# Attention over the prompt moved into the projection stage of a fused two-layer kernel, and the samples' recurrence into the prompt's recurrence stage

## The reference, cut to what matters

```python
def even_mixer(x, prev_row, S0, k_buf, v_buf, start_pos, prm, i):
    proj = x @ w_in
    pr = proj[..., :RWKV_COLS]
    ...
    mixed = pr + prm['tshift_mu'][i] * (shifted - pr)
    y_a, S = rwkv7_mixer(mixed, S0, ...)
    q, ks, vs = jnp.split(proj[..., RWKV_COLS:], ...)
    y_b, k_new, v_new = swa_mixer(q, ks, vs, k_buf, v_buf, start_pos, prm['attn_sinks'][i], prm['rel_bias'])
    out = jnp.concatenate([y_a, y_b], axis=-1) @ prm['w_out'][i]
```

## Time and profile before

| what | value |
|---|---|
| median of 3 runs | 1638.11 us (1632.55 to 1643.83) |
| the profiled execution: span of its instructions | 1637.2 us (its own time from outside is not recorded apart) |
| PE busy, mean granted clock | 1449.6 us (89%), 0.927 |
| DVE, ACT, POOL busy | 642.2, 366.8, 207.0 us |
| input transposed, from 0 to | 26.8 us |
| `project`, products, to | 331.2 us |
| `attend`, to | 448.3 us |
| `rwkv_chunks`, to | 641.4 us |
| `mix_out`, experts, pooling, experts, to | 1637.2 us |

### The profile page before, as it was taken

One profiled execution on the slowest core, in us unless ns is written; L12 is line 12 of the kernel. 1 busy time (PEld: TensorE's weight loads), 2 busy tenths in 40 slices (PEclk: granted clock), 3 DMA queues, 4 the chain that ended last, 5 costly groups with the idle time before them and its releaser, 6 DMA issues. The chain is left out here.

```text
span 1637.2 us, 26246 instructions
## 1 busy us (share of the span) xinstructions
PE 1449.6 (89%) x10111; PEld 889.8 (54%) x10112; DVE 642.2 (39%) x1022; ACT 366.8 (22%) x789; POOL 207.0 (13%) x266
## 2 busy tenths in 40 slices
PE   6999999966779998999749999994994699999968
PEld 4566666645668895445424444443794344444423
DVE  1122553069245562867551111115795211111117
ACT  1333110066523332111201111111231111111111
POOL 4000000000054332110001101005000101010040
PEclk9999999988689999999959999996797799999989
DMA  6673110041020003000378796776005688786353
GB/s 194 133 284 132 29 26 26 0 115 22 9 51 4 4 4 114 28 26 27 114 261 298 261 332 235 271 240 245 1 28 202 235 270 303 277 281 223 146 217 120
DMA packets 137055, 236.96 MB, mean 145 GB/s; under 512 B 20178, under 2 KB 100035, under 8 KB 136682
## 3 DMA queue, kind: packets, MB, share of 16 engines
q1 hardware_dynamic: 113458, 151.01, 29.0%
q0 software_dynamic: 16880, 60.49, 10.0%
q10 hardware_dynamic: 6624, 24.12, 3.7%
HBM read 178.92 MB, written 58.21 MB: 145 GB/s over the span
## 5 line engine op out<-in xcount | busy, mean ns | idle before, releaser
L2299 PE MATMUL ex_pb<-ew_w_gate_up,ex_xT 128*128 x736 | 330.0, 602 | 6.0 <-issue 3.7
L298 PE MATMUL pj_pb<-pj_xT,pj_w 128*128 128x348 f32 (+3 forms) x960 | 282.1, 455 | 0.8 <-ACT pj_xT L322 0.8
L298 PEld LDWEIGHTS pj_pb<-pj_xT,pj_w 128*128 128x128 f32 (+1 forms) x960 | 178.8, 186 | 101.9 <-ACT pj_xT L322 0.8
L2299 PEld LDWEIGHTS ex_pb<-ew_w_gate_up,ex_xT 128*128 128x128 f32 x736 | 138.0, 192 | 165.2 <-issue 164.1
L2282 PE MATMUL ex_pb<-ew_w_down,ex_hiddenT 128*128 x368 | 165.7, 593 | 3.4 <-ACT ex_hiddenT L2369 3.4
L2492 DVE TENSOR_TENSOR ex_hidden<-ex_hidden,ex_pb 128x256 f32<-128x256 f32 x46 | 19.4, 421 | 324.6 <-ACT ex_hidden L2364 324.6
L2282 PEld LDWEIGHTS ex_pb<-ew_w_down,ex_hiddenT 128*128 128x128 f32 x368 | 66.3, 190 | 69.9 <-issue 69.9
L2487 DVE COPY ex_y_rows<-ex_pb 128x512 f32<-128x512 f32 x46 | 31.8, 692 | 134.5 <-PE ex_pb L2282 134.5
L430 DVE SCALAR_TENSOR_TENSOR mixed<-pj_pb,v_mu,mixed 128x347 f32<-128x347 f32 (+3 forms) x42 | 24.0, 572 | 145.7 <-ACT mixed L372 145.6
L2364 ACT ACTIVATE ex_hidden<-ex_pb 128x256 f32<-128x256 f32 x46 | 17.7, 386 | 261.4 <-PE ex_pb L2299 261.4
L2242 POOL COPY ex_tokens_now<-ex_token_of_slot 128x1 uint32 (+1 forms) x48 | 9.6, 200 | 451.3 <-PE ex_pb L2271 399.3
(11 more groups left out here) (423 smaller groups left out, 2061.2 us busy)
## 6 DMA issues: line engine op xcount, KB each, us to landing
ew_w_gate_up<-in_w_ex_gate SPq DMA_DIRECT2D x32, 1024.0 KB, 8.4
ew_w_gate_up<-in_w_ex_up SPq DMA_DIRECT2D x32, 1024.0 KB, 11.0
ew_w_down<-in_w_ex_down SPq DMA_DIRECT2D x32, 1024.0 KB, 13.1
scratch_slots_out<-ex_y_rows ACTq DMA_DIRECT2D x46, 512.0 KB
scratch_slots_out<-pj_tmp POOLq DMA_DIRECT2D x4, 4096.0 KB, 16.0
scratch_x_stored<-x_rows SPq DMA_DIRECT2D x16, 512.0 KB
pj_w<-in_w_in SPq DMA_DIRECT2D x7, 1024.0 KB, 10.5
minus_kk_then_y<-in_x_prompt SPq DMA_DIRECT2D x8, 512.0 KB
```

The costliest lines, as they stand in the source:

```text
L298: last = nc.tensor.matmul(product(at)[:, 0:tn], w[:, s % NW, k, c0:c0 + mrows], xT[:, k, x0:x0 + tn], start=(k == 0), stop=(k == KD - 1))
L2299: last = mm(pb[:, 2 + u, :], xT[:, u, k, :], w[:, k, :], start=(k == 0), stop=(k == KD - 1))
```

## The change

`project` and `attend` become one stage, `project_attend`. The tiles are computed in another order: keys and values first (thirds 0 to 5), then queries (6 to 17), then keys of the recurrence (18 to 29), and so on; so the first 6 tiles are plain and 14 mixed ones follow. Slab 0 now holds 256 columns where it held 192, and the gathered slabs are 1 and 2. The products have two banks (4 and 5) up to third 47 and four after it. The steps of the attention are tied to the third `at` after whose products they are issued: PE's scores of block n in thirds 16 + 3n and 17 + 3n (a half of the heads each, two banks for both), the exponentials in 18 + 3n and 19 + 3n, DVE's half of the normalising in 19 + 3n and ACT's in 20 + 3n, transposes in 21 + 3n and 22 + 3n, outputs in 22 + 3n and 23 + 3n. The scores have two buffers, laid over the array of the decay sums; bias and transposed probabilities lie over the array of the rates. The samples' attention stands at single thirds from 18 to 38; the norms of the keys follow in thirds 41 to 46, decay and rate from 47. The reciprocal (L411 of before) is cut into three parts for each tile. The samples' recurrence goes into `rwkv_chunks`: its transposes and copies into step 0, its 18 DVE operations three to a step into steps 1 to 6, its loads behind the loads of `w_out` on SP. The diff, cut to its core:

```diff
-def project(nc, io, pr, A, B, U, pq, vec, keep, const):
+def project_attend(nc, io, pr, A, B, U, pq, vec, keep, const):
-    slabs = [(NR, WL + AL + GL, ((0, WL + AL, 12), (WL + AL, GL, 13)))]
-    slabs += [(HW * j, HW, ((0, P, 2 * j), (P, P, 2 * j + 1))) for j in (2, 3, 0, 1, 4, 5)]
-    slabs += [(QC + HW * j, HW, ((0, P, 14 + 2 * j), (P, P, 15 + 2 * j))) for j in range(3)]
+    slabs = [(QC + HW * j, HW, ((0, P, 14 + 2 * j), (P, P, 15 + 2 * j))) for j in (2, 0, 1)]
+    slabs += [(HW * j, HW, ((0, P, 2 * j), (P, P, 2 * j + 1))) for j in (2, 3, 0)]
+    slabs += [(NR, WL + AL + GL, ((0, WL + AL, 12), (WL + AL, GL, 13)))]
+    slabs += [(HW * j, HW, ((0, P, 2 * j), (P, P, 2 * j + 1))) for j in (1, 4, 5)]
-    Q_SLABS = (7, 8)
+    Q_SLABS = (1, 2)
+    V_ROWS = 7
+    SCORES, EXPS, TURNED = 16, 18, 21
+    S_KEYS, S_SCORES, S_ROWS, S_MAX, S_EXP, S_NORM, S_PROBS, S_OUT, S_TAKEN = (18, 21), 24, 27, 27, 29, 30, 33, 36, 38
+    SQUARES, NORMS, LORA, SMALL = 37, 41, 46, 47
+    INVERSES = tuple(42 + c if c < 9 else 43 + c for c in range(12))
+    SUMS, KEYS = (48, 50, 52, 54), (51, 55, 56, 57)
+    WIDE = 48
+        def bank_of(at):
+            return 4 + (at % 4 if at >= WIDE else at % 2)
...
@@ SP @@
+            load_slab(1)
             for v in range(KVH):
...
-            load_slab(1)
+            load_slab(2)
...
+            sp.wait_ge(s_tr, TILES)
+            sp.dma_start(kc, io["cache_swa_k"][0].rearrange("b t h d -> t b (h d)")).then_inc(q["k_in"], 16)
             sp.wait_ge(s_bw, 16)
...
+            load_slab(3)
             sp.wait_ge(q["v_tr"], 1)
...
+            load_slab(4)
...
+            for k in range(5, len(slabs)):
+                load_slab(k)
@@ PE @@
+            def prompt_attention(at):
+                n, step = of_block(at, TURNED)
+                if step == 0:
+                    transposes(n, 0)
+                    transposes(n, 1)
+                elif step == 1:
+                    transposes(n, 2)
+                    transposes(n, 3)
+                    output(n, 0)
+                    output(n, 1)
+                elif step == 2:
+                    output(n, 2)
+                    output(n, 3)
+                n, step = of_block(at, SCORES)
+                if step in (0, 1):
+                    scores(n, step)
...
+                    if at in (WIDE + 2, WIDE + 3):
+                        pe.wait_ge(q["y"], NT)
+                        pe.wait_ge(q["sy"], 1)
+                    else:
+                        before = at - 4 if at >= WIDE + 4 else at - 2
...
+                    prompt_attention(at)
+                    sample_attention(at)
...
@@ ACT, after its part of the product @@
+                    n_, step = of_block(at, TURNED)
+                    if step in (0, 1):
+                        probs(n_, 2 * step)
+                        probs(n_, 2 * step + 1)
+                    elif step == 2:
+                        take_y(n_)
+                    n_, step = of_block(at, EXPS)
+                    if step in (0, 1):
+                        exps(n_, step)
+                    elif step == 2:
+                        normalise(n_)
@@ DVE, after its part of the product @@
+                    n_, step = of_block(at, SCORES)
+                    if step in (0, 1):
+                        masked_scores(n_, step)
+                    n_, step = of_block(at, EXPS + 1)
+                    if step == 0:
+                        normalise(n_)
@@ rwkv_chunks, PE (called at six places of step 0) @@
+            def sample_rows(j):
+                if j == 0:
+                    pe.wait_ge(q["pre"], 1)
+                else:
+                    pe.wait_ge(q["rows_cp"], j)
+                for t in range(4):
+                    last = nc.tensor.transpose(pb[0:NS, 2, P * t:P * t + P], sample_cols(j, t), ident[:, :])
@@ rwkv_chunks, DVE @@
+            def samples(n, place):
+                k = 3 * (n - 1) + place
+                if 0 <= k < 18:
+                    sample_step(k // 9, k % 9)
                 if n:
                     take_a_by_state(n - 1, 1)
+                    samples(n, 0)
                 take_z(n, 2)
                 take_by_r(n, 1)
                 take_x(n, 2)
                 if n + 1 < NT:
                     take_a_by_b(n + 1)
+                if n:
+                    samples(n, 1)
                 take_z(n, 3)
                 take_x(n, 3)
                 if n + 1 < NT:
                     take_b_k_by_a(n + 1)
+                if n:
+                    samples(n, 2)
                 take_z(n, 4)
@@ rwkv_chunks, SP, behind the two loads of w_out @@
+            for j in range(6):
+                sp.wait_ge(q["rows_cp"], j + 1)
+                sp.dma_start(scr[j], vrow[j]).then_inc(q["rows_wr"], 16)
+            sp.wait_ge(q["rows_wr"], 96)
+            for half in range(2):
...
```

More of the change, by code:

```diff
@@ L204, in project @@
         s_slots = m.sem("slots_zeroed")
+        names = ("sink v_tr v_cp bias_rd sc masked neg ex inv prob_v prob_a ptr pcp o y out k0"
+                 " k_in v_in s_in kt ktc qc ssc sscc tr mx sex spr tr2 tr2c so sy").split()
+        q = {k: m.sem(f"at_{k}") for k in names}
+        n_small = 16 * (3 + 2 * NS)
         block = m.block()
@@ new lines, in take_xT, with copy_qkv @@
+        def take_xT(eng, copy, par):
+            for i in range(par, TILES, 2):
+                n = P if i < NT else 2 * NS
+                eng.wait_ge(s_tr, i + 1)
+                src = pb[:, 2 * par:2 * par + 2, :].rearrange("p b (k t) -> p (b k) t", k=4)[:, :, 0:n]
+                copy(xT[:, :, 1 + P * i:1 + P * i + n], src).then_inc(s_xT[par], 1)
+        def copy_qkv(eng, copy, at):
+            t0, _, n, _ = thirds[at % 3]
+            eng.wait_ge(s_mm, at + 1)
+            copy(pq[:, tiles[at // 3][3] - 14, 1 + t0:1 + t0 + n], product(at)[:, 1:1 + n]).then_inc(s_cp[at % 2], 1)
@@ new lines, in rate, with norm @@
+            def rate(t, cut):
+                t0, tn = cuts[cut]
+                act.wait_ge(s_small, small + 1)
+                small_taken(nc.scalar.activation(B[:, t, t0:t0 + tn], pb[:, small_bank(small), 0:tn], ACT.Sigmoid,
+                                                 bias=vec["iclr_a0"][:, t:t + 1]))
+            def norm(t, cut):
+                t0, tn = cuts[cut]
+                act.wait_ge(s_small, small + 1)
+                small_taken(nc.scalar.activation(A[:, t, t0:t0 + tn], pb[:, small_bank(small), 0:tn], ACT.Sqrt))
@@ new lines, in _ @@
+            for i, (_, _, mrows, tile) in enumerate(tiles):
+                for third, (t0, n_prompt, n, _) in enumerate(thirds):
+                    at = 3 * i + third
+                    if i < PLAIN:
+                        if at % 2:
+                            copy_qkv(dve, nc.vector.tensor_copy, at)
+                    else:
+                        dve.wait_ge(s_now, at - 3 * PLAIN + 1)
+                        mu = vec["mu"][0:mrows, tile:tile + 1]
+                        out = pr[0:mrows, tile, t0:t0 + n]
+                        last = stt(out=out[:, 0:n_prompt], in0=product(at)[:, 0:n_prompt], scalar=mu, in1=out[:, 0:n_prompt],
+                                   op0=ALU.mult, op1=ALU.add)
+                        if n > n_prompt:
+                            last = stt(out=out[:, n_prompt:], in0=product(at)[:, 1 + n:1 + n + NS], scalar=mu, in1=out[:, n_prompt:],
+                                       op0=ALU.mult, op1=ALU.add)
+                        last.then_inc(s_mix, 1)
+                    if at == V_ROWS:
+                        value_rows()
+                    n_, step = of_block(at, SCORES)
[4 more added lines that the diff above has]
+                        normalise(n_)
+                    if at == 3 * PLAIN:
+                        sample_queries()
+                    if at == S_SCORES:
+                        sample_scores()
+                    if at == S_MAX:
+                        sample_max()
+                    if at == S_NORM:
+                        sample_normalise()
+                    if at == S_PROBS:
+                        sample_probs()
+                    if at in INVERSES:
+                        inverse_norm(*divmod(INVERSES.index(at), 3))
+                    if at in SUMS:
+                        sums(SUMS.index(at))
+                    if at in KEYS:
+                        keys(KEYS.index(at))
@@ L1331, in _ @@
             last.then_inc(q["so"], 1)
+            pe.wait_ge(q["ydr"], 16)
+            pe.wait_ge(q["asc"], 2 * NT)
+            for t in range(4):
+                last = nc.tensor.transpose(pb[:, 1, NS * t:NS * t + NS], yr[:, P * t:P * t + P], ident[0:NS, 0:NS])
+            last.then_inc(q["ytr"], 1)
         @block.vector
```

869 lines of the change are left out of this document (407 added, 462 removed).

## The result

The changed kernel takes 1601.5 us (median of four, 1593.6 to 1602.9) against 1637.7 us (1632.6 to 1643.8): ratio 0.977, 95% interval 0.973 to 0.980. The forecast was 1596 us in a range of 1584 to 1614. The profiled execution has a span of 1601.1 us, 36.1 less than before and 5.6 more than the 1595.5 forecast for it.

The account below looks back on a forecast made before the run. The prediction took PE to bound the projection and the latency of a chain over three engines the attention. From 1637.2 us, -50.7 for the merging and +9.0 for the recurrence gave 1595.5, forecast as 1596, range 1584 to 1614.

Parts of the forecast that it names:

- part 3: Recurrence stage: grows by 9.0 us from taking in the samples' recurrence.
- Part 1: Attention stage: disappears from the path with one barrier, 117.1 us.
- Part 2: Merged stage: PE's attention work at full clock, switches, slab 0 and the end cost 66.4 us; net gain 50.7.
- (a): Start of the recurrence: a load of ACT's exponential table stands on the path, +1.3 us.
- (b): Recurrence step 0: six added groups of four transposes and ACT copies, +2.0 us (0 to 6).
- (d): Recurrence steps 1 to 6: 18 samples' DVE operations cost 0.7 us a step at place 0, +4.2 (0 to 22).
- (c): Recurrence step 1: DVE's operation at place 0 waits for loads through memory, +1.5 us (0 to 8).
- (e): Recurrence start: PE enters at half clock as before, 0 us (to -3.5).
- Rival 1: Recurrence stage becomes bound by DVE: 1620 us at worst, chance 0.09.
- Rival 2: Merged stage: PE waits about 3 us in thirds B and C of each block; middle 1622 us, chance 0.05.
- Rival 3: Merged stage: PE waits out each block's chain, 35 us a block instead of 20.2; 1714 us, chance 0.03.
- Rival 4: Merged stage: a semaphore puts the attention's tail behind the products; gain only 20 us, 1617 us, chance 0.03.

Follow-up runs that it names:

- run 8: Changed kernel with each block's transposes two thirds earlier, PE's scores before transposes, ACT's exponentials before copies: 1672.7 us against 1644.8 for the kernel before, single execution.
- run 1: Changed kernel with the samples' output of seven of eight samples left out: the recurrence begins at 394.57, 8.0 us earlier.
- run 2: Changed kernel with the samples' scores issued in two thirds and their output in four, nothing left out: 1596.6 us, ratio 0.974.
- run 12: Changed kernel with output spread, early table load and first-place operation in a gap, plus samples' scores in four pieces of 8: 1583.1 us, single execution.
- run 4: Changed kernel with all but two of the samples' 18 recurrence operations on DVE left out: steps 1 to 6 take 127.4 us against 136.6.
- run 5: Changed kernel with each step's first-place samples' operation moved to where DVE waits for PE, before take_x of level 3: steps 2 to 6 take 105.5 us.
- run 3: Changed kernel with the samples' 18 recurrence operations one place later: step 1 takes 21.77 us, 6.1 less.
- run 7: Changed kernel with transposes of probabilities, their products and the result's copy one third earlier per block: the recurrence begins at 406.7.

## Why the prediction was right, and where it was off

The time lay in the range, and the gain came from the mechanism that was forecast. That the miss is no more than 5.6 us is in part luck: the rest behind the recurrence gave 1.8 us back, and it differs by up to 10 us between executions of the same code. In part 3, terms put too high hid part of one that was put too low.

**What bounds the kernel** held. With the attention between the products, PE is busy throughout and waits for nothing of it. Run 8 shows the other case: take the spacing away and 45 us of waits return, with a fallen clock behind them.

**Part 1** held: the stage is gone, with its 117.1 us.

**Part 2** said 66.4 us; the stage's end moved by 45.7, so it cost 71.4. The term that failed is "Their output is 64 instructions at 0.41 us for four (434.14 to 434.55), 6.6 us", and with it the premise that the attention's work "has to be priced at the full clock". The output took 8.7, and 1.7 and 1.8 us more went into the two products behind; 5.6 us in all, shown by runs 1, 2 and 12. Without them the part comes to 65.8. The other terms held: the samples' scores 4.2 us (157.35 to 161.53), the period of a block 20.36 us (188.79 to 209.15) against 20.2, slab 0 0.8 us (27.56 against 26.8) against 1.0. Scores of a block took 2.1 us and not 1.8, inside the 4 us set aside for the switches.

The prediction also named a clock below 0.9 as the sign that PE waits. Here it fell to 0.50 in places where PE did not wait.

The warning was in the trace. The earlier trace rows show the output at 0.41 us for four; these rows follow them in the timeline of the kernel before:

```profile
434.99 0.38 PE L664 MATMUL at_pb<-at_s_probsT,projected_qkv 128*64 128x4 f32 x2
435.30 0.37 PE L665 MATMUL at_pb<-at_s_probsT,at_kv_sample 8*64 8x4 f32 x2
435.60 0.38 PE L664 MATMUL at_pb<-at_s_probsT,projected_qkv 128*64 128x4 f32 x2
```

Four take 0.61 us from here on, on a PE that had not stopped since 426.22. The prediction took the faster rows as the price and does not mention the slower ones behind them.

**Part 3** said 9.0 us and was 11.4. (a) is 1.3, right as a term: 402.61 to 403.90. (b) was put at 2.0; step 0 grew by 0.46 us. Since step 0 takes 20.2 to 21.5 us in the profiles of the changed family and no run leaves its copies out, that is a bound for (b) and not its price. (d) was put at 4.2: runs 4 and 5 give 2.7 and 3.3 us for steps 2 to 6, 3.3 to 3.9 with step 1 counted alike. Run 5 shows that it is the price of place 0; it doesn't divide it between the short slack and POOL.

(c) was put at 1.5 within 0 to 8 and is the term that failed: 2.8 us of waiting, and 3.3 us of half clock that the prediction did not have; run 3 gives 6.1 back. The wait was mis-sized in one step, the "about 2 us of landing". DVE came 7.9 us after the last copy (437.82 to 445.73), as forecast. But the last load, issued at 442.43, landed at 448.47. The loads of the values, of 8 KB each, landed in 5.9 us here and in 2.0 us before the change (the views list DMA issues, their size and, where it can be told, the median us to landing; first the kernel before, then the changed one):

```profile
at_values<-scratch_sample_scratch SPq DMA_DIRECT2D x2, 8.0 KB, 2.0
...
projected_qkv<-in_state_rwkv SPq DMA_DIRECT2D x2, 512.0 KB
...
rc_values<-scratch_sample_scratch SPq DMA_DIRECT2D x2, 8.0 KB, 5.9
```

In the kernel before, SP issued the two loads of the state (512 KB each) behind all four small loads, from 343.88 on. The change issues one ahead of each pair of small loads, at 439.31 and 441.15. That they are what delays the small ones is argued from this order, and no run tests it.

The 0.4 us for POOL within (d) can be read directly, in step 2 of the changed kernel:

```profile
472.87 1.27 POOL L1081 TENSOR_TENSOR decay_sums<-mixed,decay_sums 128x512 f32<-128x512 f32 x1
...
473.64 1.58 DVE L1452 TENSOR_TENSOR mixed<-rc_sa,rc_vectors_by_head 128x1024 f32<-128x1024 f32 x1
```

POOL ends at 474.14, DVE 1.08 us later at 475.22. At 495.33 (L1454) it is 1.40 us and again ends 1.08 us behind POOL's L1081 (494.56 + 1.09). In run 5 the same L1452 stands at 473.64 beside no POOL work and takes 1.22. The Trainium skill ("SBUF — State Buffer", Who interferes with whom) says that such a pair shuts each other out; these rows agree. The 8 us that the prediction worked out from it did not come: four of the six operations at place 0 met POOL, in its last 0.3 to 0.5 us, and lost 0.2 to 0.4 us each, 1.1 in sum.

(e) held: the recurrence starts as before, 12.64 us from the first exponential to take_z (12.63 before).

The 11.4 us as the two traces have them: 1.3 to the first exponential, 0.5 in step 0, 7.0 in step 1, 2.0 in steps 2 to 6 and 0.6 behind the last take_z of level 1. Steps 4 and 5 took 21.99 and 21.73 us already before the change, so the 2.0 are less than what runs 4 and 5 give for (d).

**The rivals.** Rival 1, the recurrence bound by DVE: DVE is busy 122 of 204 us, and in steps 2 and 3 of run 5 its added work costs nothing; it did not happen. Rival 2, PE stalled in part: run 7 takes a third away and PE still doesn't wait. Rival 3 was made in run 8. The prediction priced it at 14.8 us for a block; it measured 8.7, since only the multiply and ACT's part were waited for. It named 5.3 us of waits for a block as the point where the gain is gone, and of the clock it said only that it can add. With 5.6 the kernel is 28 us slower than before. At run 8's ratio (69.5 us for 44.6 of waits) the gain of 36 us would be gone at some 2.9 us for a block (an estimate; no run stands there). Rival 4: the last product of block 7's attention is done at 310.9, and the stage's products end at 400.2, so nothing of it stands behind them.

## What to carry to other kernels

A stage in which no engine is full can be laid into a stage in which one engine is full and the others have room. Its pieces have to be spread in two ways: by the latency of their chain, so that the full engine never meets a wait, and by their size, so that no long run of tiny matmuls stands together. An operation added to an engine that alternates with another belongs in a gap of that engine: of three operations of 1.2 us in a step, one cost 0.5 to 0.7 us at one place and nothing at another. A short wait in front of PE can cost more than its length, because the clock that falls after it comes back late: here 2.8 us cost 6.1. And a price per instruction is to be read over the whole run of them in the trace, not from its first rows.

## What was not expected of the hardware

- PE's granted clock fell to 0.50 (1.2 GHz) while PE was recorded busy 100%, in runs of matmuls of 4 columns: two groups of 16 back to back, and 64 in a row, of which the first 20 ran at full clock in one execution and the first 44 in another. Pieces of 16 records of output between products never did it, nor pieces of 8 of scores; of two groups of 16 scores in different thirds the second did it in all three runs and the first in none. Why the second isn't settled. The Trainium skill ("TensorE: Matmul & The Clock Gate", What's actually happening) ties the clock to how busy PE has been; by the busy share of these rows it would have stayed. What the array itself does within such a record no row shows.
- A wait of 2.8 us on DVE, 2.3 us on PE, cost 6.1: the clock stood at 0.50 for some 9 us afterwards, with PE 100% busy from 453 on.
- Two loads of 8 KB landed 5.9 us after their issue, issued in turn with loads of 512 KB, and 2.0 us after it where they were issued ahead of them (the kernel before). That the order is the reason isn't shown.
- The clock at the first products differs from one execution to the next: 1.00 between 27 and 60 us in five profiles of the changed family, 0.91 to 0.94 in eight, worth 1.7 to 2.2 us in the first 48 records.
- A load of ACT's table moved ahead of a barrier gained 0.5 of its 1.28 us, since ACT became the last to arrive.
